# Half an activation block in front of the transposes, and the gate products on quarters 4 to 72

## The reference

```python
def peer_ffn(x, w_query, sub_keys, down, up):
    ...
    s = jnp.einsum('thcd,cnd->thcn', q, sub_keys).astype(jnp.float32)
    sv, si = lax.top_k(s, K)
    cand_s = (sv[:, :, 0, :, None] + sv[:, :, 1, None, :]).reshape(T, H, K * K)
    cand_i = (si[:, :, 0, :, None] * PEER_NKEYS + si[:, :, 1, None, :]).reshape(T, H, K * K)
    top_s, pos = lax.top_k(cand_s, K)
    idx = jnp.take_along_axis(cand_i, pos, axis=-1)
    gate = jax.nn.softmax(top_s, axis=-1)
    ...
        a = jnp.einsum('thkd,td->thk', down[ib], xb).astype(jnp.float32)
        c = (gb * jax.nn.gelu(a)).astype(up.dtype)
        return jnp.einsum('thk,thkd->td', c, up[ib]).astype(x.dtype)
```

## Time and profile before

| what | value |
|---|---|
| median of 3 runs | 3081.79 us (3077.85 to 3085.04) |
| profiled execution | 3082.6 us, span 3080.8 us |
| TensorE busy | 3011.0 us, 98% of the span |
| VectorE busy | 1916.0 us, 62% |
| ScalarE busy | 1348.5 us, 44% |
| chain that ended last | TensorE 89%, VectorE 8%, ScalarE 2%, DMA 1% |

### The profile page before, as it was taken

One profiled execution on the slowest core, in us unless ns is written; L12 is line 12 of the kernel. 1 busy time (PEld: TensorE's weight loads), 2 busy tenths in 40 slices (PEclk: granted clock), 3 DMA queues, 4 the chain that ended last, 5 costly groups with the idle time before them and its releaser, 6 DMA issues.

```text
span 3080.8 us, 42867 instructions
## 1 busy us (share of the span) xinstructions
PE 3011.0 (98%) x17020; PEld 2624.4 (85%) x17020; DVE 1916.0 (62%) x2937; ACT 1348.5 (44%) x2134; POOL 14.8 (0%) x37
## 2 busy tenths in 40 slices
PE   8999999999999998999999999999999999999998
PEld 7768888889999886788878899988888998888996
DVE  3527998856555343499986555547575656665554
ACT  2311476454444222117745444435545544545443
POOL 0000000000000000000000000000000000000000
PEclk9999999999999999999999999999999999999999
DMA  4224455675555332345567655545554666654563
GB/s 164 90 83 162 145 178 196 221 286 192 190 191 191 106 109 81 133 137 174 181 205 273 232 191 190 190 154 179 172 182 163 187 190 182 174 180 150 149 187 123
DMA packets 222599, 528.43 MB, mean 172 GB/s; under 512 B 12810, under 2 KB 86704, under 8 KB 211440
## 3 DMA queue, kind: packets, MB, share of 16 engines
q1 hardware_dynamic: 221216, 521.10, 50.7%
q0 software_dynamic: 1232, 5.25, 0.5%
HBM read 507.42 MB, written 18.88 MB: 171 GB/s over the span
## 4 chain that ended last, share of the span: by engine, by line
PE 89%; DVE 8%; ACT 2%; DMA 1%; issue 0%; SPq 0%; ACTq 0%; POOL 0%; DVEq 0%; POOLq 0%
PE ps L2052 15%; PE ps L2036 12%; PE ps L1170 12%; PE ps L1183 11%; PE ps L1154 11%; PE ps L1120 9%; PE ps L621 3%; PE ps L637 3%; PE ps L615 2%; PE ps L1109 2%; PE ps L641 2%; PE ps L2293 1%; PE ps L572 1%; DVE arena L1607 1%; DVE arena L1599 1%; DVE arena L1597 1%
## 5 line engine op out<-in xcount | busy, mean ns | idle before, releaser
L1712 DVE TENSOR_TENSOR ring_lo<-ring,w_hi 128x1024 fp32r<-128x1024 f32 x320 | 388.5, 1224 | 270.3 <-ACT w_hi L1708 269.2
L1120 PE MATMUL ps<-h_t,ring 128*128 128x256 f32 x2048 | 466.9, 381 | 0.9 <-ACT arena L774 0.9
L1708 ACT ACTIVATE w_hi<-ring 128x1024 fp32r<-128x1024 f32 x320 | 336.7, 1057 | 268.5 <-PE ps L2052 181.8
L1120 PEld LDWEIGHTS ps<-h_t,ring 128*128 128x128 f32 x2048 | 381.4, 191 | 48.6 <-issue 1.3
L1170 PE MATMUL ps<-h_t_lo,down_hi 128*128 128x256 f32 x1024 | 288.2, 281 | 0.0
L1170 PE MATMUL ps<-h_t_expert,down_lo 128*128 128x256 f32 x1024 | 287.8, 281 | 0.0
L1170 PE MATMUL ps<-h_t_expert,down_hi 128*128 128x256 f32 x1024 | 286.8, 280 | 0.0
L2036 PE MATMUL ps<-h_t_hi,w_hi 128*128 128x256 f32 x928 | 259.9, 280 | 2.7 <-ACT arena L1851 2.7
L2036 PE MATMUL ps<-h_t_lo,w_hi 128*128 128x256 f32 x928 | 261.5, 282 | 0.0
L2036 PE MATMUL ps<-h_t_hi,ring_lo 128*128 128x256 f32 x928 | 259.6, 280 | 0.0
L1516 DVE TENSOR_TENSOR up_lo<-ring,up_hi 128x2048 fp32r<-128x2048 f32 x64 | 146.7, 2292 | 101.1 <-ACT up_hi L830 101.1
(11 more groups left out here) (417 smaller groups left out, 6145.8 us busy)
## 6 DMA issues: line engine op xcount, KB each, us to landing
ring<-in_peer_down SPq DMA_DIRECT2D x128, 1024.0 KB, 5.0
ring<-in_peer_up SPq DMA_DIRECT2D x68, 1024.0 KB, 4.8
ring<-in_w SPq DMA_DIRECT2D x132, 512.0 KB, 3.7
ring<-in_peer_up SPq DMA_DIRECT2D x120, 512.0 KB, 4.3
ring<-in_w_in SPq DMA_DIRECT2D x100, 512.0 KB, 3.7
ring<-in_w_in SPq DMA_DIRECT2D x20, 1024.0 KB, 6.4
arena<-late_gates SPq DMA_DIRECT2D x16, 1024.0 KB, 7.3
ring<-in_w_out SPq DMA_DIRECT2D x8, 1024.0 KB, 6.5
```

The source lines that it names most:

```text
L1120: m = pe.e.matmul(PS[:, act_bank(b), j * T:(j + 1) * T], RING[:, b % 2, j * D + kc * P:j * D + (kc + 1) * P], HT[:, kc, :], start=kc == 0, ...
L1708: a.e.activation(W_HI[:, g % HI_SLOTS, :], RAW[:, g % RAW_SLOTS, :], ACT.Copy).then_inc(*a.count(f"c{g}_hi"))
L1712: v.e.tensor_tensor(RAW_LO[:, g % RAW_SLOTS, :], RAW[:, g % RAW_SLOTS, :], W_HI[:, g % HI_SLOTS, :].bitcast(F32), ALU.subtract).then_inc(* ...
```

## The change

Quarters 0 and 1 of block 13 are issued in front of the wait for `hkr` and the transposes, instead of behind them; the loop behind the transposes begins its quarters at 2. `QUARTER` becomes 4, 5, ... 14, 16, ... 72: `sums(0)` stands behind quarter 4 instead of 2, `sums(62)` and `sums(63)` stay behind quarters 71 and 72, and a quarter is skipped in front of s = 11, 22, 32, 43 and 54. `LATE_BY` follows from `QUARTER` by its own formula: 0, 2, 4, 6, 8, 10, 11, 13, ... instead of 1, 3, 5, 7, 8, 10, 12, 14, ... The places of `act_out` in ScalarE's list follow in the same way.

```diff
--- before.py
+++ after.py
@@ -51,7 +51,7 @@
 REACH = [(0, 0, 1, 16), (16, 1, 3, 8), (40, 4, 4, 4), (56, 8, 8, 1)]
 REACHED = 64
 LEAD = HELD // 2 - 3
-QUARTER = [2 + s * (4 * (HELD - LEAD) - 4) // SUMS for s in range(SUMS)]
+QUARTER = [4 + s * (4 * (HELD - LEAD) - 6) // SUMS for s in range(SUMS)]
 LATE_BY = [sum(QUARTER[2 * n + 1] <= 4 * i + 4 for n in range(GROUPS_OF_TOKENS)) for i in range(HELD - LEAD)]
 LATE_BY[-1] = GROUPS_OF_TOKENS
 WHOLE = [0]
@@ -1128,13 +1128,16 @@
                     act_quarter(b, q)
             for b in range(2):
                 pe.e.wait_ge(*pe.at(f"act_ev{b}"))
+            for q in range(2):
+                act_quarter(LEAD, q)
             pe.e.wait_ge(*pe.at("hkr"))
             for t in range(TT):
                 for c in range(3):
                     m = pe.e.transpose(PS[:, t, c * P:(c + 1) * P], HKR[:, t, c, :], IDENT)
                 m.then_inc(*pe.count(f"hk_t{t}"))
             for n in range(4 * (HELD - LEAD)):
-                act_quarter(LEAD + n // 4, n % 4)
+                if n >= 2:
+                    act_quarter(LEAD + n // 4, n % 4)
                 for s in range(SUMS):
                     if QUARTER[s] == n:
                         sums(s)
```

## The result

| | before | after |
|---|---|---|
| median of 20 runs each | 3082.59 us (3077.66 to 3085.14) | 3086.64 us (3082.12 to 3091.70) |
| ratio | | 1.0014, 95% interval 1.0008 to 1.0020 |
| profiled execution, span | 3080.8 us | 3080.3 us |
| gate stage, layer 0 / layer 1 | 170.02 / 170.01 us | 170.89 / 170.89 us |

The change makes the kernel 0.14% slower: less than the 0.2% taken as a bound, but clear of noise. The gate stage is here the stretch from the end of activation block 12 on TensorE to its first output product. The two spans alone would mislead: the profiled execution after is shorter although both of its gate stages are longer. The last part of the experiments says why.

The account below looks back on a forecast made before the run. The ScalarE and VectorE ring, 4.94 us a round, was taken to set the gate stage's end. 0.11 + 2 x 0.42 = 0.95 us per layer, +1.9 in two, on the median 3081.79 gave 3083.7 us; range 3077.5 to 3088.5.

Parts of the forecast that it names:

- a ring that hands the gain back: Gate stage: ScalarE and VectorE pace each group, so 4.38 us saved per layer return as waits before gate products.
- The gap and the half clock go: Around the transposes: 2.69 us of TensorE idle vanishes, and the 24 instructions behind take about 5.2 us at clock 1.00.
- VectorE's chain starts 0.52 us later: Behind the transposes, which end at 342.49 instead of 341.97 us; bounds 0 and 0.76 us.
- Product 0 ends at the same instant, after a wait of 0.9: First gate product: TensorE waits about 0.9 us for group 0's high parts, ending at 349.29 against 349.30 us before.
- The ring keeps 4.94 us: Gate stage: ScalarE and VectorE rounds stay 4.94 us each, since none of their instructions is removed or shortened.
- +0.11 at the start, +0.42 at each of two skips, 0.95 per layer: Gate stage: first addition 0.11 us later, skips before products 11 and 43 0.42 us each, 0.95 us per layer.
- +1.9 us in two layers: Whole kernel: both layers' gate-stage delays together make it 1.9 us slower, nothing that can be measured.
- the gain is kept: Rival: the gate stage ends 4.38 us earlier in each layer, giving 3073.0 us; chance 0.08.
- The clock falls in the gate stage: Rival: small TensorE waits bring half clock, 3097 us if once per four groups, 3087 for a single stretch; chance 0.05.

Follow-up runs that it names:

- ring_before: Kernel before, with ScalarE's copy of sums 2n-2 moved in front of the scaling of group n; stage 167.32 us in layer 0, ratio 0.9990 to before.
- even_skips: Changed kernel with skipped quarters in front of products 12, 22, 32, 44, 54, all first halves of a group; stage 170.18 us in layer 0, ratio 0.9999 to before.
- spread_only: Kernel before with only the new product places, quarters 4 to 72, nothing moved before the transposes; stage 172.51 us in layer 0, ratio 1.0025 to before.
- delay_control: Kernel before plus about 0.86 us of empty TensorE work per layer before the first output product; stage 170.42 us, ratio 1.0010 to before.
- tail_before: Kernel before with products behind quarters 2 to 73, eight skips, nothing moved before the transposes; stage 168.49 us in layer 0, ratio 0.9992 to before.
- prefix_only: Changed kernel with the old product places, quarters 2 to 72, so only the half block moves; stage 172.47 / 171.78 us, ratio 1.0015 to before.

## Why the prediction was right

The forecast was 3083.7 in a range of 3077.5 to 3088.5, "nothing that can be measured" with 0.2% as the bound. Measured were 3086.6, +0.14%. Twenty executions of each did measure a difference, and 1.9 us lies under its interval of 2.5 to 6.2; the total is inside the range because that leaves 3 us for scatter. The mechanism, a ring that hands the gain back, is what the runs show. By its steps:

- **The gap and the half clock go.** Right: no idle, 5.35 us for the 24 instructions, clock 1.00.
- **VectorE's chain starts 0.52 us later.** Scaling of group 0 came 0.57 later.
- **Product 0 ends at the same instant, after a wait of 0.9.** 0.96, and 0.09 later.
- **The ring keeps 4.94 us.** Right, and ring_before shows that it was the bound. But TensorE stands close behind it: with the ring shortened, its list takes over.
- **+0.11 at the start, +0.42 at each of two skips, 0.95 per layer.** 0.16, 0.40 (5.34 - 4.94) twice, 0.87 in the first profile, 0.95 in the second.
- **+1.9 us in two layers.** This is the term that is off against the medians, which moved by 4.05. The stage accounts for 1.75 of it in the profiles compared. What was missed is that half clock behind the gap is not a fixed part of the kernel before: the sum took the profiled execution, where product 0 was held to 10.87 us by it, for all of them. Without it the same sum gives about 0.5 more per layer, 2.8 us. So the 0.11 for the start of the ring came out right with some luck: it holds against an execution in which half clock had already delayed product 0, and is about 0.5 against one at full clock. The prediction also held all half clock elsewhere to be the same in both kernels; the granted clocks speak against that, as told above.

The rivals: "the gain is kept" fell with even_skips and ring_before. "The clock falls in the gate stage" did not come about: 26 short waits in two layers, and one of 0.96 in each, left it at 1.00. The oscillation that the Trainium skill, TensorE: Matmul & The Clock Gate, A second HAM failure mode, describes for frequent micro-idles was not seen in any of these stages. The other rule cited, the Trainium skill, Perfetto Trace Analysis, Optimization Strategies, was right in its second half: what paid was the engine that TensorE waits for (2.7 us per layer), not the filling of TensorE's idle time (none).

## What to carry to other kernels

An idle gap on the chain of waits is worth closing only if the work that follows can use the time: look for the next handshake of the other engines, and measure its beat over many rounds before booking the gap. When a ring of two engines sets the end of a stage, ask three things: which instruction of the ring can be done while an engine waits, where in the round the bounded engine's extra work falls (between two halves of a group it cost 0.4 us; between groups nothing in even_skips, but about 0.5 per skip once the ring was shortened), and how much of that engine's own work stands behind the last round.

## What was not expected of the hardware

The clock after one and the same gap. About 2.7 us of TensorE idle in front of the transposes was followed by 0.50 in both layers of the kernel before and of ring_before, and by 1.00 in both layers of spread_only, delay_control and tail_before, although TensorE's list is the same in all five up to the third quarter behind the transposes. The wait of 4.42 us in prefix_only brought 0.50 in both layers. Waits of 0.96 us at product 0 brought none, in both layers of ten profiles. So a gap of that middle size costs half clock in some executions and not in others, and one profile does not tell.
